# A fused three-layer transformer kernel on one core: later rotation and scans in the middle attention, and pooled products split out of their PSUM banks in the first layer

## The reference, cut to what matters

```python
def even_mixer(h, ...):                       # first layer
    q, k, v, u = split(h @ w_in)              # 8 query heads, 2 key/value heads, u: 4 groups of 128
    ya = windowed_gqa(rope(q), rope(k), v, sink)
    yb = multiscale_pool(u, w_pool, pool_scale)   # windowed means, (mean - u) @ w_pool[g], times pool_scale
    return concatenate([ya, yb]) @ w_out

def odd_mixer(h, ...):                        # middle layer
    cq, ckv, kr, xr, xg = split(h @ w_in)
    q = rmsnorm(cq) @ w_uq ; kv = rmsnorm(ckv) @ w_ukv
    yc = dense_mla(qn, rope(qr), kn, rope(kr), v)     # 8 heads, dense softmax over 512 keys
    yd = rglru_block(xr, xg, ...)             # two gated linear recurrences, forward and backward,
    return concatenate([yc, yd]) @ w_out      # summed and multiplied by gelu(xg)

for layer in (even, odd): x = x + mixer(rmsnorm(x)); x = x + relu(rmsnorm(x) @ w1)**2 @ w2
# then a third layer with its own mixer, and a last norm
```

## Time and profile before

| what | value |
|---|---|
| device time, three runs | 1510.99, 1516.53 and 1516.61 us, median 1516.53 |
| profiled execution, its own time | 1512.91 us |
| its span, first to last instruction | 1511.1 us |
| mean granted TensorE clock | 0.991 |
| TensorE busy | 1453.9 us, 96% |
| VectorE, ScalarE, GpSimd busy | 792.1, 605.5, 569.7 us (52%, 40%, 38%) |
| memory traffic | 128.7 MB, 85 GB/s over the span |
| first layer's attention loop | first scores at 45.07 us of the span, last values at 159.44 |
| middle layer's attention loop | first scores at 624.59 us of the span, last values at 727.20 |

### The profile page before, as it was taken

The page is one execution under the profiler, slowest core; times in us unless marked ns, Lnnn a source line. Parts: engine busy times, 40 slices in busy tenths (PEclk is TensorE's granted clock), DMA queues, the critical chain, the costliest instruction groups (busy, mean ns, idle before and its releaser), DMA issues.

```text
span 1511.1 us, 20392 instructions
## 1 busy us (share of the span) xinstructions
PE 1453.9 (96%) x7122; PEld 1141.4 (76%) x7122; DVE 792.1 (52%) x1389; ACT 605.5 (40%) x1104; POOL 569.7 (38%) x236
## 2 busy tenths in 40 slices
PE   6988999999999999889999999999999999999996
PEld 5666878888888888455778888888877877776785
DVE  6885542223444578877452222444467547676434
ACT  5343432232222345855432223222253435654432
POOL 3322354444444444311344444444425642222441
PEclk9999999999999999989999999999999999999998
DMA  5211222222222222200222222222213331111221
GB/s 215 70 61 52 98 98 97 97 96 99 97 97 97 98 84 70 70 29 29 70 84 97 97 97 97 98 97 97 97 56 126 128 110 57 57 59 53 70 70 56
DMA packets 36624, 129.55 MB, mean 86 GB/s; under 512 B 4048, under 2 KB 4176, under 8 KB 36560
## 3 DMA queue, kind: packets, MB, share of 16 engines
q1 hardware_dynamic: 35136, 124.80, 24.4%
q10 hardware_dynamic: 1424, 3.90, 0.7%
HBM read 126.58 MB, written 2.10 MB: 85 GB/s over the span
## 4 chain that ended last, share of the span: by engine, by line
PE 55%; issue 27%; POOL 11%; DVE 5%; ACT 2%; POOLq 0%; DVEq 0%; ACTq 0%
PE bank L648 15%; PE bank L650 15%; PE bank L649 15%; POOL w L631 11%; PE bank L753 3%; PE bank L773 3%; PE bank L788 2%; PE bank L1086 1%; PE bank L717 0%; DVE rms L1641 0%; ACT tmp L1253 0%; ACT arena L1400 0%; PE bank L706 0%; DVE opC L1609 0%; DVE arena L2184 0%
## 5 line engine op out<-in xcount | busy, mean ns | idle before, releaser
L631 POOL TENSOR_TENSOR w<-raw,w 128x1024 fp32r<-128x1024 f32 x232 | 569.5, 2458 | 908.4 <-ACT w L1195 526.9
L648 PE MATMUL bank<-opC,w 128*128 128x512 f32 x624 | 253.2, 406 | 13.9 <-DVE opC L1609 10.5
L650 PE MATMUL bank<-opC,w 128*128 128x512 f32 x624 | 245.0, 393 | 0.0
L649 PE MATMUL bank<-opC,w 128*128 128x512 f32 x624 | 244.5, 392 | 0.0
L1773 DVE TENSOR_TENSOR mlp_op<-arena,mlp_op 128x512 fp32r<-128x512 f32 x64 | 144.5, 2260 | 188.7 <-ACT mlp_op L1310 188.7
L1282 ACT ACTIVATE w<-raw 128x1024 fp32r<-128x1024 f32 x126 | 133.1, 1057 | 239.5 <-PE bank L650 239.5
L648 PE MATMUL bank<-mlp_op,w 128*128 128x512 f32 x544 | 212.2, 390 | 3.1 <-ACT arena L1400 1.4
L650 PE MATMUL bank<-mlp_op,w 128*128 128x512 f32 x544 | 211.7, 389 | 0.0
L649 PE MATMUL bank<-mlp_op,w 128*128 128x512 f32 x544 | 211.7, 389 | 0.0
L648 PE MATMUL bank<-opA,w 128*128 128x512 f32 x416 | 162.7, 391 | 2.3 <-DVE arena L1768 1.4
L1766 DVE TENSOR_TENSOR tmp<-tmp,rms 128x512 f32<-128x512 f32 x64 | 51.5, 804 | 211.0 <-ACT tmp L1290 210.5
(11 more groups left out here) (221 smaller groups left out, 1922.9 us busy)
## 6 DMA issues: line engine op xcount, KB each, us to landing
raw<-stream_dram SPq DMA_DIRECT2D x232, 512.0 KB, 3.4
out_t_dram<-arena SPq DMA_DIRECT2D x8, 256.0 KB, 2.1
x<-x_t_dram SPq DMA_DIRECT2D x4, 256.0 KB, 5.7
x<-x_t_dram ACTq DMA_DIRECT2D x4, 256.0 KB, 7.1
rope<-ropes_dram ACTq DMA_DIRECT2D x2, 512.0 KB, 6.7
con<-consts_dram ACTq DMA_DIRECT2D x1, 993.5 KB, 8.0
arena<-p_t_dram ACTq DMA_DIRECT2D x1, 512.0 KB, 3.8
par<-params_dram ACTq DMA_DIRECT2D x1, 253.5 KB, 3.8
```

The lines of the kernel that those rows point to most:

```text
L631: pool.tensor_tensor(w_lo[:, j, :], raw[:, j, :], w_hi[:, j, :].bitcast(F32), ALU.subtract).then_inc(lo_made, 1)
L648: pe.matmul(out, wh, hi, start=first, stop=False)
L649: pe.matmul(out, wh, lo, start=False, stop=False)
L650: return pe.matmul(out, wl, hi, start=False, stop=last)
```

## The change

Four edits are made together.

1. **Pooled products.** ScalarE makes the high part of a pooled tile straight from the product's bank, with `pool_scale` as the scale, in `between_even` of the step in which the product is made, behind that step's exponentials and copies. VectorE then makes the low part in one instruction from the same bank (bank times scale minus high part) in the place where it evacuated the bank, after a wait for a new semaphore `pooled_hi`. The tile `pooled_y`, VectorE's L1608 on it and its four entries in `SPLITS` go, and TensorE waits for pooled operands by `z_ready`.
2. **Fill-in products of the middle loop.** `o_pace` begins 2, 1, 1, 1, 1, 3, 1, 1 in place of 2, 2, 2, 1, 1, 1, 1, 1. qr1 is finished in step 3 and not in step 2; step 5 holds the second product of qn2, kn2 and the first of qn3. From step 6 on nothing of it differs.
3. **Second rotation.** Step 5 and not 3, on TensorE and VectorE.
4. **Scans and what hangs on them.** Scans in steps 4, 7, 8, 10, 11; sums in 6, 9, 12; gates in 6 (both `lru` 0 and 1), 9, 12; splits in 7 (both), 10, 13. In `SPLITS` attention group 0 of the middle layer now stands ahead of `lru` 0 and 1.

```diff
-          ("xc", (0, 1)), ("ckv", 1), ("xc", (2, 3)), ("lru", (0, 1)), ("mattn", (0,)), ("lru", (2,)),
+          ("xc", (0, 1)), ("ckv", 1), ("xc", (2, 3)), ("mattn", (0,)), ("lru", (0, 1)), ("lru", (2,)),
...
-    return (2, 2, 2, 1, 1, 1, 1, 1, 2, 2, 2, 2, 2, 2, 3, 3, 2, 2, 2)[step]
+    return (2, 1, 1, 1, 1, 3, 1, 1, 2, 2, 2, 2, 2, 2, 3, 3, 2, 2, 2)[step]
...
-                need_split(*what)
+                if what[0] == "pooled":
+                    pe.wait_ge(z_ready, TILE0["pool"] + what[1] + 1)
+                else:
+                    need_split(*what)
...
-                if step == 3:
+                if step == 5:
                     rotate(7, mla["qr"][1], TILE0["mv"] + 7, c("rot_mla"), P, 1)
...
-                        if stage == "pool":
-                            act.wait_ge(z_ready, TILE0["pool"] + i + 1)
-                            hi_of("pooled", i, pooled_y[i])
 
             def between_even(step):
+                for stage, i in E_DONE[step]:
+                    if stage == "pool":
+                        t = TILE0["pool"] + i
+                        act.wait_ge(acc_full, t + 1)
+                        nc.scalar.activation(splits["pooled", i][0], bank[6 + t % 2][:, :], ACT.Copy,
+                                             scale=g("pool_scale", i)).then_inc(pooled_hi, 1)
...
-                for j in {5: (0, 1), 9: (2,), 13: (3,)}.get(step, ()):
+                for j in {7: (0, 1), 10: (2,), 13: (3,)}.get(step, ()):
                     act.wait_ge(src_ready, 8 + j + 1)
                     hi_of("lru", j, z1(8 + j))
...
-                    if stage == "pool":
-                        lo_of("pooled", i, pooled_y[i])
...
-                        TS(pooled_y[i], src[:, :], g("pool_scale", i), None, ALU.mult).then_inc(z_ready, 1)
+                        hi, lo = splits["pooled", i]
+                        dve.wait_ge(pooled_hi, i + 1)
+                        STT(lo, src[:, :], g("pool_scale", i), hi.bitcast(F32), ALU.mult, ALU.subtract).then_inc(z_ready, 1)
...
-                if step == 3:
+                if step == 5:
                     rotate(7, mla["qr"][1], P, 1, (more[:, 2, :], more[:, 3, :]))
-                if step in (1, 5, 7, 9, 11):
-                    lru_scan(3 + (1, 5, 7, 9, 11).index(step))
-                if step in (2, 8, 12):
-                    lru_sum((2, 8, 12).index(step) + 1)
-                for j in {4: (0, 1), 8: (2,), 12: (3,)}.get(step, ()):
+                if step in (4, 7, 8, 10, 11):
+                    lru_scan(3 + (4, 7, 8, 10, 11).index(step))
+                if step in (6, 9, 12):
+                    lru_sum((6, 9, 12).index(step) + 1)
+                for j in {6: (0, 1), 9: (2,), 12: (3,)}.get(step, ()):
                     lru_gate(j)
-                for j in {5: (0, 1), 9: (2,), 13: (3,)}.get(step, ()):
+                for j in {7: (0, 1), 10: (2,), 13: (3,)}.get(step, ()):
                     lo_of("lru", j, z1(8 + j))
```

8 lines of the change are left out of this document (4 added, 4 removed).

## The result

| | before | after |
|---|---|---|
| median of the runs, us | 1513.92 (four, 1510.99 to 1516.61) | 1498.07 (four, 1497.96 to 1498.23) |
| ratio after / before, 95% interval | | 0.9891 [0.9873, 0.9908] |
| profiled execution: time, span, us | 1512.91, 1511.1 | 1497.96, 1496.2 |
| TensorE busy, mean granted clock | 1453.9 us, 0.991 | 1448.4 us, 0.994 |
| first layer, scores of step 10 to scores of step 12, us | 19.61 (104.28 to 123.89) | 14.15 (106.43 to 120.58) |

The forecast was 1499.0 us, the result 1498.07. The two places that the change touches give 5.46 and 10.13 us, 15.6 together, where the sum said 15.2. Between them (scores of step 12 to the middle layer's scores 0) both kernels take 500.7 us, so nothing is given back there.

A forecast was written before the change was run, and what follows sets the result against it. TensorE, busy 96% of the span, was taken as the bound: its matmuls plus its waits. Gains of 5.9 (first layer) and 9.3 (middle layer) make 15.2 us, from a mean of 1514.3 to 1499, range 1492 to 1507.

The forecast's parts named there:

- The walk through ScalarE's chain: Middle layer, step 6: copy and splits leave ScalarE's chain ahead of the values, whose 3.67 us wait falls to 0.1.
- First layer: 5.9 taken: First layer, steps 10 and 11: gain from the pooled wait and slow products going, 5.9 us, bounds 4.4 to 6.4.
- the step that failed: First layer, step 9: ScalarE's two high parts wait for their products before the next exponentials, so the pair costs nothing.
- the 0.4 for the drain: Both layers, 0.4 us each: extra gain because the shown idle leaves out the drain of the pipeline.
- Middle layer: 9.3 taken: Middle loop: 7.0 from step 3 plus 5.2 from step 6, less 3.3 of new waits, plus 0.4: 9.3 us, between 6.5 and 12.
- the new waits: Middle loop: waits the new order brings at scores 2, qn3's product, steps 7 to 9 and scores 12, 3.3 us in sum.
- what goes: Middle loop: the waits and slow stretches of steps 3 and 6 that disappear, 12.6 us if no new wait shows.
- half of the rotation's 1.05 (640.89 less 639.84), 0.5: Middle layer, step 3: the rotation counted as part of the slow stretch behind its wait, 0.5 us of gain.
- The collision in step 6: Rival, middle layer: GpSimd's block starts before VectorE's second gate and holds it, 2.1 to 5.9 us less gain; chance 0.15.
- VectorE as the bound: Rival, middle steps 7 to 12: VectorE's backlog makes scores wait over 3.1 us four times, 1524 us; chance 0.03.
- waits not on the path: Rival, whole kernel: something other than TensorE's waits takes the time, so no change, 1511 to 1517 us; chance 0.05.
- Only one layer delivers: Rival: a long wait creeps back in one of the two layers, gain 9.5 or 6, 1504 to 1508 us; chance 0.10.

The follow-up runs named there:

- scans_alone: The changed kernel with the middle layer's fill-in products and second rotation put back, its scans still moved: 1501.80 us, ratio 0.9905 to the kernel before.
- best: The changed kernel with first-layer output products and rotation later, and middle-layer v tiles copied ahead of two weight copies: 1500.39 us, ratio 0.9905 to the kernel before.
- first_only: The kernel before with only the pooled-products edit of the first layer: 1510.72 us, ratio 0.9967 to the kernel before.
- middle_only: The kernel before with only the three middle-layer edits (fill-in products, rotation, scans): 1504.26 us, ratio 0.9933 to the kernel before.
- changed_again: The changed kernel run once more, unaltered, in a later group: 1497.93 us, ratio 0.9888 to the kernel before.
- split_first: The kernel before with only VectorE's order changed, low parts of the pooled tiles ahead of the rotation: 1508.35 us, ratio 0.9960 to the kernel before.

## Why the prediction was right, point by point

**Which waits go.** Right in all three places: L1608 is off the list, the rotation's product in the middle loop has no wait in the view, and the values of step 6 wait for nothing (0.1 foreseen). The walk through ScalarE's chain held: its last copy there is at 650.10, with the table load at 647.38 directly behind the roots.

**First layer: 5.9 taken, 5.46 measured,** a term mis-sized. The first output product was to start 0.2 us later; it starts 5.56 us after the scores of step 10 (106.43 to 111.99), where it was 5.00 (104.28 to 109.28). Of the 0.56, 0.17 is the foreseen part. 0.14 lies between the start of ScalarE's pair and the output product (110.40 to 111.99, foreseen 108.00 to 109.45): ScalarE's bank copy with a scale takes 0.63 in the pair and not the 0.59 of the copy without one, and VectorE starts 0.16 after the first copy ends (111.03 to 111.19). The other 0.25 comes from the step that failed: "in step 9 the two high parts wait for their products ... so that pair costs nothing". VectorE waits there 0.80 and 0.30 us for ScalarE's 0.69, so its masking of step 10 begins 1.58 us after the scores (108.01 - 106.43), and ScalarE's exponentials, at 108.66, wait 1.43 us for that and come 2.23 us after the scores; they were at 1.97 before. Before, VectorE was idle for 0.40 us ahead of its second bank, and the masking began 1.06 us after the scores. The wait came out as 2.08 and not 1.7. The bound of 4.4 to 6.4 held the gain. The 5.9 was also a choice more than a sum: its terms give 5.7, and 6.1 with the 0.4 for the drain.

**Middle layer: 9.3 taken, 10.1 measured.** The mechanism was right; the new waits were put too large, and what goes too large as well. Predicted in sum 3.3; measured, from waits and the lengths of steps: scores 2 0.71 (0.7 foreseen), qn3's product 0.16 (0.5), step 7 up to scores 8 0.26 (0.65), step 8 0.49 (6.04 us where step 9 takes 5.55; 0.35 and 0.5 foreseen), step 11 up to scores 12 0.53 (0.6). That is 2.15. The walk let the backlog of VectorE's steps 6 and 7 pile up by whole instructions, while that engine had slack between them (1.35 us at 652.20, ahead of step 6's masking). The scores of step 5 also waited 0.47 before, which had not been counted and is gone.

What goes was put at 12.6 us (7.0 + 5.2 + 0.4) and measures 11.85 from step to step: 3.3 in step 2 (8.80 us from scores 2 to scores 3, where 3.83 and a product of 0.69 and a rotation of 0.95, from the changed kernel, make 5.47), 3.2 in step 3 (8.08 against 4.86) and 5.3 in step 6 (10.17 against 4.87). The term that was mis-sized is "half of the rotation's 1.05 (640.89 less 639.84), 0.5". The rotation was not slow: the granted clock over it was still 1.00, it takes 1.05 in scans_alone behind a wait of 0.68, and 0.95 in the changed kernel (642.24 to 643.19) behind none.

```profile
639.80:640.90 1.10, 1.06 (x3) 0.30 (x4) 1.06 (x2) 1.10 (x2) 0.00 (x0) 1.00 0.00 0
640.90:643.00 2.10, 2.10 (x7) 0.61 (x8) 0.81 (x2) 1.37 (x3) 1.88 (x1) 0.56 0.00 0
```

(The kernel before; the granted clock is the third number from the end.) The rest is the 0.4 for the drain, of which some 0.1 is found. 11.85 + 0.47 - 2.15 is 10.17, and the loops differ by 10.13.

**How much of it was luck.** That 15.2 came within 0.4 us of the 15.6 is in part luck: the first layer was put 0.4 too high and the middle one 0.8 too low, and in the middle layer 0.8 too much gain stood against 1.15 too much in new waits and 0.5 not counted. The time came within 1 us also because the mean of four scattered executions (1514.3) happened to lie near the 1513.92 beside which the changed kernel was measured; from the median shown ahead the sum gave 1501.3.

**Rivals.** The collision in step 6 did not come: the second gate starts near 656.9 and GpSimd at 657.28. That is 0.4 us and not the 1.0 of my walk, so its 0.15 was not too much. In best the same race was lost by 0.07 us. VectorE as the bound and "waits not on the path" fell with the first trace. "Only one layer delivers" fell with first_only and middle_only.

**The rule on waits** was wrong: "a wait of over 3 us costs about twice what it shows, and a short one only itself". The error did not show in the sum, since the slow stretches that went were read from the trace and not from the rule, and since the changed kernel's profiled execution had none behind its 2.08. It had one behind step 9's short waits, so that a granted clock of 1.00 in both loops, which the prediction wanted to see, did not come true (0.72 in the window 98 to 104). Two lines of windows, of the changed kernel and then of changed_again, show it:

```profile
98.00:104.00 6.00, 5.27 (x27) 3.85 (x28) 5.41 (x15) 4.38 (x13) 2.37 (x1) 0.72 0.00 0
106.00:118.00 12.00, 9.92 (x59) 6.41 (x58) 8.69 (x24) 7.86 (x19) 2.38 (x1) 1.00 0.14 45
```

```profile
98.00:104.00 6.00, 4.92 (x32) 3.51 (x32) 6.00 (x19) 4.75 (x14) 2.41 (x1) 1.00 0.00 0
106.00:118.00 12.00, 9.92 (x52) 6.47 (x51) 7.52 (x22) 6.67 (x18) 2.36 (x1) 0.86 0.16 54
```

The same program has its stretch at half clock in step 9 in one execution and in step 10 in the other. That also closes the balance of the two profiled spans, 1511.1 and 1496.2. Of the 15.6 us gained, 3.0 are lost again in slow stretches in steps 0 and 9 of the first layer that the kernel before's execution did not have, although it had the same waits there (2.25, 1.58 and 0.55), 1.4 gained behind the middle layer where that one had a stretch (clock 0.95 from 1390 to 1410) and this one none, and 0.9 gained ahead of the first scores: 14.9. The forecast of 1499 from the mean of the four executions shown, and not from the one profiled, allowed for this scatter without knowing where it comes from.

## What to carry to other kernels

Where TensorE waits for another engine, ask first what stands ahead of the late instruction in that engine's order and whether it can stand behind: split_first got 5.3 of its layer's 5.5 us with the same instructions, and edit 4, which only reorders, 6.1 of the middle layer's 10.1 us. Price a wait of some 2 us as itself plus a chance of 1.4 to 3.2 us more for the clock, so one that goes from 3 to 1 is worth more than the 2. Before moving work, list for each two-SBUF-input instruction of VectorE how far GpSimd's next block is away: margins of 0.07 and 0.4 us decided 2 us each here, and a change that helps one step (the v tiles in best) can lose more by what it makes late.

## What the runs showed of the hardware

**The clock.** TensorE's granted clock fell to half (1.2 GHz) behind waits of as little as 1.61 and 0.55 us, 2.2 in sum (step 9), and not behind 2.08 in the same execution. With the same wait it did in one execution and not in another. A stretch costs 1.4 to 1.7 us, in four cases 3.1 to 3.2, without relation to the wait (behind 3.15 us of wait 3.2 in two executions and 1.5 in a third). The Trainium skill, page "TensorE: Matmul & The Clock Gate", section "What's actually happening", says that the monitor behind the clock runs freely and doesn't start with the kernel, so that the place of a change varies between runs; the traces agree that it varies, for the drop as well, by the two pairs of windows above, and no run shows the cause. The stretches are also the likely source of the scatter of both kernels (1510.9 to 1517.2 and 1495.5 to 1498.6): the mean granted clock of an execution goes with its time, 0.997 at 1495.46 and 1495.77 against 0.994 at 1497.93 to 1498.6, and 0.991 at 1510.94 against 0.988 at 1517.23. Where the stretches lie was seen only in the executions that have a profile.

**The port.** A VectorE instruction with two SBUF inputs that begins behind GpSimd's block is held until the block ends: 0.07 us behind it, 2.85 us instead of 0.69 (best). Where it began 0.4 us ahead (117.90 in the changed kernel) it took its 0.69, and GpSimd's block 2.54. A TENSOR_SCALAR between SBUF tiles was held as well: two normalizations of 0.88 us together took 2.05 at 636.36, over GpSimd's block from 635.35, in the changed kernel. Between its steps 2 and 4 that hid behind slack and cost nothing.
